# The context's output product, second norm and first queries move from the front phase into the opening of the first expert layer, one block of 128 tokens at a time

## The reference

```
layer 0:  h, hc = modulate(rms_norm(x)), modulate(rms_norm(ctx))
          hc @ w_in -> latents, keys, values, gated conv (31 taps)
          yc  = concat(attention, silu(layer_norm(conv))) @ w_out        # "output product"
          ctx = ctx + modc[2] * yc
          hc2 = modulate(rms_norm(ctx), modc[3], modc[4])                # "second norm"
          ctx = ctx + modc[5] * peer_ffn(hc2)                            # experts
          the same for x, with attention over context and own keys
layer 1:  HGRN2 mixer, then peer_ffn for x only, final norm

peer_ffn, per token and for each of 8 heads:
          q = x @ w_q            (256 per head, in two halves of 128)    # "queries"
          s = q . sub_keys       (128 scores per half)                   # "scores"
          16 best of each half -> 16 best of their 256 sums -> 16 experts
          act = gelu(x . u[e]);  y += gate * act * v[e]
```

## Time and profile before

| | |
|---|---|
| runs | 2542.82, 2543.28, 2547.66 us; median 2543.28 |
| the profiled execution's own time | 2544.54 us |
| its span | 2542.5 us |
| busy | PE 1966.6, DVE 1671.9, ACT 1160.0, POOL 885.4 us |
| DMA | 954.32 MB, mean 375 GB/s |
| gathers (queue 0) | 847.30 MB, 79.9% of the 16 engines' time |

### The profile page before, as it was taken

The page is one execution under the profiler, slowest core; times in us unless marked ns, Lnnn a source line. Parts: engine busy times, 40 slices in busy tenths (PEclk is TensorE's granted clock), DMA queues, the critical chain, the costliest instruction groups (busy, mean ns, idle before and its releaser), DMA issues. The chain is left out here.

```text
span 2542.5 us, 31830 instructions
## 1 busy us (share of the span) xinstructions
PE 1966.6 (77%) x10908; PEld 942.4 (37%) x10908; DVE 1671.9 (66%) x4157; ACT 1160.0 (46%) x3157; POOL 885.4 (35%) x808
## 2 busy tenths in 40 slices
PE   8999887878786767777777776889997676666766
PEld 5667432443341212333333331568752221122110
DVE  1634689887667667767586857473557666666655
ACT  2342456776545444544354534412335444444444
POOL 0001344545434444434343434200115444444342
PEclk8999998888997878888988888899998877788676
DMA  9554999999999999999999999795169999999997
GB/s 365 207 191 134 423 422 418 399 403 414 425 425 426 426 426 426 426 425 426 425 414 426 414 426 426 291 369 186 64 239 411 426 426 426 426 426 426 427 426 306
DMA packets 146995, 954.32 MB, mean 375 GB/s; under 512 B 16529, under 2 KB 22161, under 8 KB 45329
## 3 DMA queue, kind: packets, MB, share of 16 engines
q0 software_dynamic: 113472, 847.30, 79.9%
q1 hardware_dynamic: 33360, 104.98, 11.2%
HBM read 951.17 MB, written 1.05 MB: 375 GB/s over the span
## 5 line engine op out<-in xcount | busy, mean ns | idle before, releaser
L1079 PE MATMUL pY<-uv,diag 64*64 64x512 f32 x6144 | 994.2, 741 | 500.7 <-ACT diag L1155 476.2
L960 POOL DMA_INDIRECT uv<-uv_dram,idx x768 | 860.5, 1120 | 1288.0 <-PE pY L1079 1037.7
L1313 DVE SCALAR_TENSOR_TENSOR uv<-uv,H 128x1024 f32<-128x1024 f32 x768 | 940.0, 1224 | 545.2 <-DMA uv<-uv_dram,idx 526.2
L1079 PEld LDWEIGHTS pY<-uv,diag 64*64 64x64 f32 x6144 | 194.3, 152 | 1128.3 <-ACT diag L1155 977.3
L1147 ACT ACTIVATE gelu<-dots 128x1 f32<-128x1 f32 x768 | 154.8, 202 | 867.3 <-DVE uv L1313 856.9
L1155 ACT ACTIVATE diag<-cst,coef 128x128 f32<-128x128 f32 x768 | 308.3, 401 | 70.9 <-ACT coef L1151 0.4
L1151 ACT ACTIVATE coef<-gelu,gate 128x1 f32<-128x1 f32 x768 | 226.3, 295 | 28.4 <-ACT gelu L1147 0.7
L983 PE MATMUL pqs<-hT,wring 128*128 128x256 f32 x512 | 127.4, 405 | 0.7 <-ACT S L1130 0.7
L983 PEld LDWEIGHTS pqs<-hT,wring 128*128 128x128 f32 x512 | 101.0, 202 | 43.6 <-issue 29.5
L134 PE MATMUL plh<-hT,wring 128*128 128x256 f32 (+1 forms) x512 | 101.7, 360 | 8.8 <-DMA wring<-hg_zz_dram 6.2
L1147 ACT ACT_TABLE_LOAD x79 | 101.4, 1283 | 1.4
(11 more groups left out here) (448 smaller groups left out, 2246.6 us busy)
## 6 DMA issues: line engine op xcount, KB each, us to landing
aw<-ada_w_dram POOLq DMA_DIRECT2D x12, 2048.0 KB, 8.8
wring<-peer_q_dram SPq DMA_DIRECT2D x36, 512.0 KB, 10.3
uv<-uv_dram,idx POOLq DMA_INDIRECT x768
wring<-hg_zz_dram SPq DMA_DIRECT2D x24, 512.0 KB, 8.9
wring<-w_in_dram SPq DMA_DIRECT2D x16, 512.0 KB, 9.6
arena<-hg_zz_dram SPq DMA_DIRECT2D x16, 512.0 KB
arena<-ada_w_dram POOLq DMA_DIRECT2D x4, 2048.0 KB
h_aw<-ada_w_dram POOLq DMA_DIRECT2D x4, 2048.0 KB
```

What stands on the lines that cost most here:

```text
L960: nc.gpsimd.indirect_dma_start(out=uv[:, n % SLOTS, :], out_offset=None, in_=t[f"uv{l}"], in_offset=bass.IndirectOffsetOnAxis(ap=idx[:, s ...
L1079: last = nc.tensor.matmul(pY[crossed(own, half), b, half * 512:(half + 1) * 512], diag[own, n % DIAGS, own], uv[own, n % SLOTS, D + half * ...
L1313: v.scalar_tensor_tensor(out=uv[:, j, 0:D], in0=uv[:, j, 0:D], scalar=1.0, in1=H2[:, own, :], op0=ALU.mult, op1=ALU.mult, accum_out=dots[: ...
```

## The change: what it does

The front phase ends when the mixer's concatenated output `mixc` is ready. What followed there (the product with `w_out`, the residual, the second norm) is done by a new class, `ContextOutput`, in the opening of the first expert layer, for block 0 (tokens 0 to 127) and block 1 apart. The search for step 1 leaves the opening: it runs beside picks 0 to 7, and that for step 2 beside picks 8 to 15. Head 1's queries and scores go beside picks 1, 3 and 6. Modulation group 14 moves into the attention loop, group 15 behind the transposes of the attention output, and `mod_finish` for the parts 2 to 5 waits for all 16 groups. The second half of `w_out` is loaded into the `uv` slots 6 and 7, so gather 6 waits for block 1's product. x's first two remaining `w_in` tiles are loaded once block 1's sum of squares is made (they share space with the squares). `peer_q0`'s first four tiles are loaded in the opening. The warming matmuls before the picks go from nine to three; the four at the end of the front stay.

```
@@ front_phase
-            for i in range(KT):
-                load_tile(sp, "w_out", i, first[2] + i)
-            lin_ahead(sp, 2)
+            lin_ahead(sp, 1)
...
-                if u < len(UNITS) and u % 2 == 0:
+                if u % 2 == 0:
                     modulate(6 + u // 2)
...
-            for i in range(2):
-                tile(2, i, range(4))
...
-            for k in range(KT):
-                if k == 6:
-                    modulate(14)
-                pe.wait_ge(r_sq, k + 1)
-                last = mm(A[0][:, 0:T], ones[:], h1[:, k, :], start=(k == 0), stop=(k == KT - 1))
-            last.then_inc(r_sum, 1)
             modulate(15)
             turn(14)
             turn(15)
             keep_warm(nc, po[:], cst, 4)
...
-            mod_finish(fin, 0, (2, 3, 4, 5), ...)
             (reciprocal, four products for the conv's norm)
-            (outputs, norm, hT)
             dve.wait_ge(m_turned, GROUPS)
+            mod_finish(fin, 0, (2, 3, 4, 5), ...)
             mod_finish(fin, 1, (0, 1), ...)
@@ peer_phase
+            opening.sync_late(sp)
             for h in range(HEADS_AHEAD):
                 weights(h)
+            opening.sync_queries(sp)
+            if l == 0:
+                sides[0].sync_first(sp)
...
+            opening.tensor(pe)
             pe.wait_ge(rows_copied, 2 * BLOCKS)
-            keep_warm(nc, pY[:, 1, 0:512], cst, 9 if l == 0 else 3)
+            keep_warm(nc, pY[:, 1, 0:512], cst, 3)
...
-            for s in range(1 if opening else AHEAD):
-                for part in range(TOPK):
-                    topk(s, part)
+            opening.vector(dve)
+            for part in range(TOPK):
+                topk(0, part)
+            opening.second(dve)
@@ class ContextOutput
+        def products(b, tiles):
+            for i in tiles:
+                n, g = KT * b + i, self.out_first + i
+                (wait for wring's tile i, or for all four late tiles)
+                if n >= 4:
+                    pe.wait_ge(self.x, n - 3)
+                for k in range(KT):
+                    last = mm(self.bank(n), w[:, k * P:(k + 1) * P], self.mixc[:, k, self.cols(b)], ...)
+                last.then_inc(self.product, 1)
...
+        products(0, range(KT))
+        products(1, range(RING))
+        sums(0)
+        queries(0, self.pq)
+        scores(0)
+        products(1, range(RING, KT))
+        rows(0)
+        sums(1)
+        queries(1, self.pt)
+        rows(1)
+        scores(1)
...
+    def norm(self, dve, b):
+        dve.wait_ge(self.summed, b + 1)
+        v.tensor_scalar(self.rs[b], self.b[b][:, 0:P], 1.0 / D, EPS, ALU.mult, ALU.add).then_inc(self.scaled, 1)
+        dve.wait_ge(self.root, b + 1)
+        v.reciprocal(self.rs[b], self.rs[b]).then_inc(self.scaled, 1)
+        v.tensor_tensor(hT of the block, xT of the block, rs broadcast, ALU.mult).then_inc(self.y, 1)
+        (gain and shift for k = 1, 3, 5, 7; ACT has the even ones)
+    def vector(self, dve):
+        self.residual(dve, 0)
+        self.norm(dve, 0)
+        self.residual(dve, 1)
+        dve.wait_ge(self.x, 2 * KT)
+        dve.sem_inc(self.acc_free, RING)
+    def second(self, dve):
+        self.norm(dve, 1)
```

More of the change, by code:

```diff
@@ L311, in front_phase @@
             sem(f"f_{x}") for x in ("ot", "ote", "csum", "cstep", "csq", "croot", "cmix"))
-        r_out, r_sq, r_sum, r_rs, r_root, r_y = (sem(f"f_r_{x}") for x in ("out", "sq", "sum", "rs", "root", "y"))
         block = c.enter_context(nc.Block())
@@ L1059, in _ @@
                     late = h + HEADS_AHEAD == HEADS
-                    if (b, k) == ((1, 2) if late else (0, 9 if opening and s == 0 else 4)):
+                    if (b, k) == ((1, 2) if late else (0, 9 if s == 0 else 4)):
                         queries(h + HEADS_AHEAD, 0)
@@ L1893, in __init__, with rest_load, sync_first @@
         self.x_used, self.x_taken = sem("tm_x_used"), sem("tm_x_taken")
+    def rest_load(self, sp, i):
+        sp.dma_start(self.H2[:, i % 2, :], self.t["w_in"][4 + i]).then_inc(self.x_loaded[i % 2], 16)
+    def sync_first(self, sp):
+        sp.wait_ge(self.opening.summed, 2)
+        for i in range(2):
+            self.rest_load(sp, i)
     def rest_end(self, p):
@@ L1899, in sync @@
     def sync(self, sp, n):
[L1901 to L1905 removed]
+        for i in range(2, 2 * self.REST):
+            if n == self.START + 4 * (i - 1):
+                sp.wait_ge(self.x_used, i - 1)
+                self.rest_load(sp, i)
         for i in range(KT):
```

309 lines of the change are left out of this document (160 added, 149 removed).

## The result

| | before | after |
|---|---|---|
| median of the runs (18 of each) | 2544.33 us | 2556.14 us |
| lowest, highest | 2536.58, 2551.84 | 2550.28, 2561.53 |
| ratio of the medians, 95% interval | | 1.0045 [1.0036, 1.0055] |
| profiled execution: time, span | 2544.54, 2542.5 | 2561.3, 2559.5 |
| PE, DVE, ACT, POOL busy | 1966.6, 1671.9, 1160.0, 885.4 | 1976.8, 1673.2, 1165.8, 878.0 |

The change costs 11.5 us (0.45%, from 9 to 14). The forecast was 2546.3 with a range up to 2550.5: too low by 10 us (the change was to cost 3.0 us, so 8.5 of them belong to the change; the rest is mostly that the kernel before came out 1 us above the three runs that the forecast started from). The profiled execution is 17 us longer than the one before.

The account below looks back on a forecast made before the run. It took the first expert layer as bound by an always-full DMA queue, so only the first gather's instant counts: 244.47 to 247.5, +3.0 on 2544.54, giving 2547.5, or 2546.3 us on the median's footing. Range 2540.5 to 2550.5.

Parts of the forecast that it names:

- What bounds the kernel: First expert layer: a DMA queue that never runs dry; the change is worth what it moves the first gather, at 244.47 us.
- The front's tail: End of front to PE's product: warming matmuls on the path, 6.2 us at low clock; product starts at 197.3, 14.6 later.
- From product to first gather: Opening: tiles 21.4, sums 1.8, norm 3.3, queries 5.5, scores 1.3, four tiles 7.1, search 9.4; first gather 247.5, 3.0 later.
- The sum's upper bound: First gather at 251.1, +6.6 us, with low clock through the warming matmuls, queries and start of the four tiles.
- Loads: Two query tiles move into the full stretch, two `w_in` tiles ahead of it; 2.5 us each, zero in sum.
- The first picks: After the first gather: eight slots cover PE, some 4 us to spare at gather 11, about 26 us after; costed at nothing.
- The sign to look for: No window under 400 GB/s from 255 us; wrong if windows from 265 to 290 us show DMA share under 0.95.
- C: First picks: the queue runs dry because pick 3 frees slot 3 too late, delaying gather 11; 2551 to 2555, chance 0.08.
- B: Opening: low clock everywhere, into the four last tiles; +6.6 us, 2549.9, chance 0.12.
- A: Opening: the clock holds or the warming matmuls are quick; gather at 243 to 244.5, 2542.3, chance 0.15.
- D: Opening: search starts on block 0's scores, or the front's tail is short; -4 to -8 us, 2538.0, chance 0.08.
- E: Product: narrow matmuls bound by the weight load, 0.3 us each; +10 us, 2556, chance 0.02.

Follow-up runs that it names:

- Experiments 1: Changed kernel with warming earlier: the front's four warming matmuls go ahead of the last turns, where PE waited; 1.0014 of the kernel before.
- experiment 2: Changed kernel without the four warming matmuls at the end of the front; 1.0029 of the kernel before.
- experiment 4: Changed kernel with the tiles later: SP loads head 3's keys and two query tiles behind pick 12, not ahead of x's third `w_in` tile; 1.0022 of before.
- experiment 5: Kernel before, with head 3's keys and two query tiles issued straight ahead of x's third `w_in` tile instead of before the picks; 0.9996 of before.
- experiment 6: Changed kernel with DVE's search for step 0 ahead of block 1's last four residual sums; 1.0042 of the kernel before.
- experiment 3: Changed kernel where PE, in block 1's first four product tiles, no longer waits for the tile just issued; 1.0039 of the kernel before.
- Experiment 8: The sums between, with nine or no warming matmuls instead of three ahead of layer 0's picks; nine 0.9998, none 0.9985 of the kernel before.
- experiment 9: Kernel before, with three warming matmuls instead of nine ahead of the picks; 0.9988 of before.
- three edits: Changed kernel with warming earlier, head 3's query tiles behind pick 12, and no PE wait on its own product; 0.9997 of the kernel before.
- four edits: The three edits plus the search for step 0 ahead of block 1's last four residual sums; 0.9990 of the kernel before.
- the sums between: The three edits, with block 1's last four residual sums set behind the search's third, sixth, ninth and twelfth parts; 0.9985 of the kernel before.

## Why the prediction was wrong

**What bounds the kernel.** "The change is worth what it moves that one instant", plus any hole. The direction came out of it: of the 13.0 us that the bytes are late at 140 MB, 7.0 are the instant. But the instant was not the only one to sum to: eight slots make the first gathers independent of PE, and all after them follow PE. That the engines show 1.00 in the earlier trace rows does not say that the gathers are far ahead. And the queue of the kernel before is not one that "never runs dry": of its 268 windows of 5 us between 260 and 1600 us, 17 lie under 400 GB/s, and against 426 GB/s they all lose 19 us together (after the change 23 windows and 25.5 us). The slices of the earlier trace rows are too coarse for this, and the sign "no window under 400 GB/s" would have failed in the kernel before.

**The front's tail: right.** Start of the product forecast at 197.3 (15.6 us after the zero, if the attention is 1.3 us late), measured 195.91 (16.1 after it); 0.5 us too little from zero to start. The 1.3 us did not show: the zero of the eleven profiles with the new front lies at 178.2 to 181.4, of the three with the old at 177.7 to 180.4. The low clock in the warming matmuls: 6.2 forecast, 6.39 measured. Experiments 1 and 2 show what they cost.

**From product to first gather: the term mis-sized.** Forecast 50.2 us, measured 250.52 - 195.91 = 54.6. Twelve tiles and their waits 24.2, not 21.4: PE's wait on its own product, 1.9 for four tiles, and 0.52 for the late half of `w_out`, which I had at nothing; the rest is 0.228 us a matmul instead of 0.223. That wait is in the diff's new class; I read the order of the instructions and not what stands between them. Queries 6.5, not 5.5; norm 3.6, not 3.3; sums 2.0, not 1.8; copy and scores 1.0, not 1.3; block 1's four tiles 7.3, not 7.1. The search took its 9.4. Together with the start, +6.6 us where +3.0 stood: 3.6 of the 8.5 us by which I was wrong. The sum's upper bound was added up wrongly, 250.9 and not 251.1; the measured 250.52 lies just under it although the product started at 195.91 and not at the bound's 198.5, with the clock low in the warming matmuls and the queries but not in the four last tiles, and two waits that the bound had not.

**Loads: the bytes right, the place not.** "Two tiles of 0.52 MB each way ... zero in sum." The bytes do sum to nothing. But SP is a queue. Head 3's two tiles wait for head 1's scores, which the change puts beside pick 6, and so they go out right ahead of the third `w_in` tile, which PE needs at pick 11. The wait itself delays that tile by 0.5 us only (it was issued 18.75 us after pick 0; in experiment 4, where nothing stands ahead, 18.3), the two tiles by some 10 (it landed 17.9 us after its issue, in experiment 4 8.0). I looked for what moved past the first two `w_in` tiles and not for what stood ahead of the next.

**The first picks: the step that failed.** It is the term that stood at zero: "I cost this part at nothing; the cover is the eight slots, with some 4 us to spare at gather 11." Gather 11 came 27.7 us after the first, near the 26 forecast. But I stopped there. Gather 19 came 56.3 us after the first, before it was 49.2, and eight gathers of 2.46 us and the other tiles do not cover that. Experiment 4 takes this loss away (5.9 us by the ratios, 3.3 in the bytes), experiment 5 shows that it needs a PE that frees the slot late (1.4 us lost for a wait of 10.5), experiment 6 that it grows when the gathers alone are put forward (7.7 us). The sign to look for was set too early: the windows from 265 to 290 us show a share of 1.00 to 1.03, the hole is at 305 to 315.

**The rivals.** C said what happened (the queue runs dry in the first picks; 2551 to 2555, against 2556.14) and had 0.08. That its number is near is partly luck, for it had 5 to 9 us for the hole alone, which took 3.3: its place was gather 11 with PE at half speed, the true one gather 19 with PE at full speed but without a gap, then waiting for a load. B's low clock is there in the warming matmuls and the queries, but not in the four last tiles (7.31 us). A fell with the 6.39 and 6.53 us of warming matmuls and queries, D with the first MAX8 at 241.13. E: 0.228 us for a narrow matmul against the 0.3 it needed. The Trainium skill (TensorE: Matmul & The Clock Gate, LDWEIGHTS) makes the weight load a cost by its own columns; here sixteen half tiles take 7.38 + 7.41 + 7.31 + 7.31 = 29.4 us (with experiment 3's row for the third four), eight whole ones 27.86. That is 1.5 us or 6% more, where the estimate in the prediction was 9 to 13 us; at 128 columns the load is hidden but for at most that.

**What stays open.** Some 2.7 us of the profiled difference arise between 90 and 100 MB, at 485 to 495 us, behind queries at the low clock. The kernel with the tiles later loses 2.5 us between 90 and 100 MB too, after winning 1.7 between 50 and 80; the one with warming earlier loses 0.3 there. No experiment was aimed at it. Experiment 8 gives 3.3 us for 5.0, which the intervals neither tell from all nor, by themselves, from nothing. And a kernel before whose third `w_in` tile alone is late, without the early pair of experiment 5, was not run.

## What to carry to other kernels

Where a queue of N slots feeds an engine chain, sum two paths to the same place: to the first transfer, and to the first slot that comes free behind the last gap of the consumer. The later of the two decides; here the first transfer came 8.0 us earlier by itself and the time did not change measurably (experiment 6). Follow each moved load to the next one behind it in its queue, with the waits that it takes along. Warming matmuls are free only in a wait that exists: on the path four of them cost 4.9 us and gave 2.6 back (experiment 2), ahead of pick 0 six of them fitted in a wait but for 0.8 us (experiment 9).

## What the runs showed of the hardware

- The clock behind an idle is not a property of the program. Block 0's queries, 16 matmuls of 128 columns, stand behind an idle of 3.59 us in all eleven profiles of the new order, and took 3.81 us in two, 5.43 or 5.44 in five, 6.3 to 6.5 in four. Five of these kernels have the same program up to this place (three edits, four edits, and the three with the sums between): 6.31, 6.34, 3.81, 6.32 and 5.44 us. In the three profiles of the old order they took 6.59 to 6.69 behind 3.40 us, which would have looked like a rule. What decides is open.
- A PE wait on a semaphore that its own last matmul raises costs 0.5 us a tile (2.33 us from start to start against 1.81, 1.9 us for the four in experiment 3), though its row shows 0.30 us of idle. The Trainium skill (TensorE: Matmul & The Clock Gate, Single matmul latency) gives a formula by which, as an estimate, a lone bf16 matmul of 128 columns takes 0.22 us at the full clock; an fp32 matmul is two records here, and no run measured a lone one.
- A `w_in` tile of 0.5 MB that SP issues into the full stretch right behind two query tiles landed 17.7 (before, the first one), 17.9 (changed, the third) and 18.4 us (experiment 5, the third) later. With no query tiles ahead of it the third one landed after 8.0 us (experiment 4) and 8.1 us (the sums between). One of 0.5 MB behind two others in the same queue thus came 10 us later, where the bytes of two such tiles are 2.5 us of DMA time.
